# Linear attention mixer: scored queries turned back by four transpositions against a reordered identity

## What is computed

```python
def step(S, inp):
    qc, kc, vc, gc = inp                        # chunks of 16 positions
    G = jnp.cumsum(gc, axis=1)
    qg = qc * jnp.exp(G)
    att = jnp.einsum('blhd,bshd->bhls', qg, kc * jnp.exp(-G))
    att = jnp.where(causal, att, 0.0)
    o = jnp.einsum('bhls,bshv->blhv', att, vc) + jnp.einsum('blhd,bhdv->blhv', qg, S)
    g_last = G[:, -1]
    S = S * jnp.exp(g_last)[..., None] + jnp.einsum('bshd,bshv->bhdv', kc * jnp.exp(g_last[:, None] - G), vc)
    return S, o
```

## Time and profile before

| what | before |
|---|---|
| median of 3 runs | 2017.05 us (2014.43, 2017.05, 2022.57) |
| span of the profiled execution, the only time the profile gives for it | 2015.7 us |
| TensorE busy (matrix passes) | 1951.5 us, 97% |
| TensorE busy (weight loads) | 1763.9 us, 88% |
| VectorE, ScalarE, GpSimd busy | 62%, 46%, 50% |
| DMA | 324.64 MB, mean 161 GB/s |

### The profile page before, as it was taken

One profiled execution on the slowest core, in us unless ns is written; L12 is line 12 of the kernel. 1 busy time (PEld: TensorE's weight loads), 2 busy tenths in 40 slices (PEclk: granted clock), 3 DMA queues, 4 the chain that ended last, 5 costly groups with the idle time before them and its releaser, 6 DMA issues.

```text
span 2015.7 us, 35615 instructions
## 1 busy us (share of the span) xinstructions
PE 1951.5 (97%) x13890; PEld 1763.9 (88%) x13890; DVE 1244.4 (62%) x2220; ACT 930.6 (46%) x1557; POOL 1008.8 (50%) x1249
## 2 busy tenths in 40 slices
PE   7999999999999999999999999999999999999997
PEld 5998989798888988897889999999998889989976
DVE  5988342426887787755147777777454157874552
ACT  3676522334555555342354444443243347674333
POOL 4776704026555655250356666566631337776602
PEclk8999999999999999999999999999999999999998
DMA  4444476535444544487353444444586344445870
GB/s 130 149 147 135 135 250 231 208 105 174 124 116 132 151 132 140 138 297 241 113 170 108 130 130 130 137 136 146 165 313 211 132 148 141 135 148 166 292 231 27
DMA packets 332615, 324.64 MB, mean 161 GB/s; under 512 B 19768, under 2 KB 313056, under 8 KB 332448
## 3 DMA queue, kind: packets, MB, share of 16 engines
q1 hardware_dynamic: 330944, 321.49, 49.8%
q10 hardware_dynamic: 1504, 0.87, 0.2%
HBM read 292.16 MB, written 29.61 MB: 160 GB/s over the span
## 4 chain that ended last, share of the span: by engine, by line
PE 75%; DVE 14%; ACT 5%; issue 2%; DMA 2%; POOL 1%; SPq 1%; DVEq 0%; ACTq 0%
PE ps L773 10%; PE ps L774 10%; PE ps L778 10%; PE ps L1458 5%; PE ps L1467 4%; PE ps L1261 3%; PE ps L1524 2%; PE ps L888 2%; PE ps L763 2%; PE ps L765 2%; PE ps L764 2%; ACT wh L1713 2%; DVE work L2543 2%; PE ps L1602 1%; PE ps L1541 1%
## 5 line engine op out<-in xcount | busy, mean ns | idle before, releaser
L1693 POOL TENSOR_TENSOR wl<-raw,wh 128x256 fp32r<-128x256 f32 x1216 | 1003.3, 860 | 979.1 <-ACT wh L1713 978.9
L1713 ACT ACTIVATE wh<-raw 128x1024 fp32r<-128x1024 f32 x304 | 311.8, 1053 | 202.1 <-PE ps L778 49.8
L773 PE MATMUL ps<-Hh,wh 128*128 128x320 f32 x1200 | 372.2, 324 | 2.8 <-DVE work L2563 0.9
L774 PE MATMUL ps<-Hl,wh 128*128 128x320 f32 x1200 | 360.4, 314 | 0.0
L773 PEld LDWEIGHTS ps<-Hh,wh 128*128 128x128 f32 x1200 | 230.0, 192 | 11.3 <-DVE work L2427 2.3
L774 PEld LDWEIGHTS ps<-Hl,wh 128*128 128x128 f32 x1200 | 230.4, 192 | 2.1
L2258 DVE TENSOR_SCALAR work<-ps 128x512 f32<-128x512 f32 (+8 forms) x220 | 100.3, 474 | 170.9 <-PE ps L871 39.8
L778 PE MATMUL ps<-Hh,wl 128*128 128x320 f32 x1200 | 201.1, 310 | 0.0
L778 PEld LDWEIGHTS ps<-Hh,wl 128*128 128x128 f32 x1200 | 183.2, 189 | 0.1
L773 PE MATMUL ps<-Oh,wh 128*128 128x320 f32 x512 | 152.2, 310 | 3.7 <-DVE Ol L3004 3.7
L774 PE MATMUL ps<-Ol,wh 128*128 128x320 f32 x512 | 151.1, 308 | 0.0
(11 more groups left out here) (439 smaller groups left out, 3922.0 us busy)
## 6 DMA issues: line engine op xcount, KB each, us to landing
raw<-rg_w_in SPq DMA_DIRECT2D x128, 256.0 KB, 3.5
raw<-hg_w_in SPq DMA_DIRECT2D x128, 256.0 KB, 4.8
raw<-ssd_w_in SPq DMA_DIRECT2D x96, 256.0 KB, 3.9
work<-cache_mem_k SPq DMA_DIRECT2D x40, 512.0 KB, 6.3
work<-cache_mem_v SPq DMA_DIRECT2D x40, 512.0 KB, 5.1
raw<-rg_w_out SPq DMA_DIRECT2D x64, 256.0 KB, 3.6
raw<-x_w_k SPq DMA_DIRECT2D x64, 256.0 KB, 3.6
raw<-x_w_v SPq DMA_DIRECT2D x64, 256.0 KB, 3.7
```

The source lines that it names most:

```text
L773: pe.matmul(ps[:, bank, 0:n], high(half, k), mh[:, k, 0:n], start=(k == 0), stop=False)
L774: pe.matmul(ps[:, bank, 0:n], high(half, k), ml[:, k, 0:n], start=False, stop=False)
L1693: ins = pool.tensor_tensor(out, src, wh[:, parted(n) % HALVES, r:r + 2].bitcast(F32), ALU.subtract)
L1713: act.activation(wh[:, nx.n % HALVES], raw[:, slot, :, half * P:(half + 1) * P], ACT.Copy).then_inc(hi_ready, 1)
```

## The change

The four products of line 1302 become four transpositions (one line further down, line 1303, since a line is added). Each writes 128 columns in place of 64. The columns of the identity are reordered, so that the 64 wanted ones come first and the 64 unwanted ones behind them; the next product starts 64 columns further on and overwrites the unwanted ones. For that the high half is now done before the low one in each tile. The unwanted columns of the last tile are columns 256 to 319 of bank 4, of which the samples' product overwrites partitions 0 to 63. Number and place of the instructions in the program, waits and signals stay as they are.

```diff
-                    own = ident[:].rearrange("p (g r) -> p g r", g=4)[:, :, 0:16]
+
+                    own_first = ident[:].rearrange("p (g a r) -> p a g r", g=4, a=2)
                     for T in range(2):
-                        for low in range(2):
+                        for low in (1, 0):
                             at = T * P + 64 * (1 - low)
-                            pe.matmul(ps[:, 4, at:at + 64], hg_sq[:, T, P * low:P * low + P], own, start=True, stop=True)
+                            pe.matmul(ps[:, 4, at:at + P], hg_sq[:, T, P * low:P * low + P], own_first, start=True, stop=True, is_transpose=True)
                     pe.matmul(ps[0:64, 4, 256:320], hg_ks[:, h, :], hg_q[i % 2][:, h, SEQ:NT], start=True, stop=True).then_inc(S("hg_att_full"), 1)
```

## The result

| | before | after |
|---|---|---|
| median of 6 runs | 2016.18 us (2012.97 to 2022.57) | 2003.13 us (2000.39 to 2006.66) |
| ratio | | 0.9939, 95% interval 0.9923 to 0.9955 |
| span of the profiled execution | 2015.7 us | 2001.6 us |
| stretches at granted clock 0.50 inside the mixer ("slow stretches") | 9 | 4 |

The change makes the kernel 13 us faster, 0.6%, against 5.2 us forecast and a range that ended at 2004.5. I start where the page of the changed kernel differs.

What follows compares the result with a forecast made beforehand. PE's instruction stream was taken to bound the mixer. 6.4 us saved by sixteen shorter turnings back, less 1.2 us lost at waits, gives 5.2 us: 2017.05 - 5.2 = 2011.8 us, range 2004.5 to 2019.0.

Steps and rivals of the forecast that it cites:

- The price of the instructions: Turning back in the mixer: four transpositions take 0.53 us against 0.93, saving 0.40 us per head, 6.4 us for sixteen.
- The dear and the cheap end of the bounds: Price of a transposition in the turning back: 0.22 us each saves 1.1 us in all, 0.055 us each saves 9.0.
- the clock: Half-clock stretches in the mixer, 1.5 us each, get redrawn: three more or fewer, 4.5 us either way, middle unmoved.
- What is given back: PE arrives earlier at three waits for the weights' low part in the mixer: 3 x 0.40 = 1.2 us lost.
- transpositions count as rest: Rival: turning back draws new half-clock stretches; eight give 2023.9 us, sixteen 2035.9. Chance 0.10, 0.04 for over 0.5%.
- the passes would be as dear as before: Rival: new transpositions take two passes each or stall on overlapping columns; gain 1.1 us or less, 2016 us. Chance 0.10.
- the chain binds in every period: Rival: the states' chain bounds every mixer period, 3.2 us waited away, 3.2 left: 2013.9 us. Chance 0.10.
- More than forecast: Rival: cheap end's 9.0 us, or 5.2 us plus three half-clock stretches fewer, 9.7: 2007.4 us. Chance 0.13.

Runs made afterwards that it cites:

- the clear pair: Kernel before and changed kernel, each with 8-column products filled to 32 columns and SyncE's weight block ahead of the store: 1998.01 us and 1993.66 us.
- the 64-column run: Kernel before with the samples' 8 products of 8 columns widened to 64 columns each: 2007.2 us, ratio 0.9952.
- moving the load: Changed kernel with SyncE issuing the fourth weight block of a group ahead of the store of head 1's states: 2000.04 us, ratio 0.9921.
- the changed kernel with both edits: Changed kernel with 8-column products filled to 32 columns and SyncE's weight block ahead of the store: 1993.66 us, ratio 0.9891.
- the widened changed kernel: Changed kernel with the samples' 8-column products widened to 64 columns: 2002.6 us, ratio 0.9921.

## Why the prediction was right or wrong

**The price of the instructions was right.** Starts 0.11 us apart, 0.53 us in all, 6.4 us for sixteen; the clear pair shows 6.3. The dear and the cheap end of the bounds were both wrong. The factor of four that I quoted from the Trainium skill ("TensorE: Matmul & The Clock Gate", section "Terms"), read as four against the same product, isn't what these rows show: a transposition in float32 takes 0.11 us, half of the 0.22 of a two-pass product.

**The step that failed is the clock.** It stood in the sum with nothing and was allowed 4.5 us either way; it measured 7.5 us. I wrote that "shifting PE by 0.4 us a head will redraw them", three more or fewer, and that it "doesn't move its middle". I treated the nine stretches as a draw with the same mean before and after. They have different means: 9 and 12 in the old loop, 4 and 5 in the new, five fewer by the granted clock of all executions as well, which is 7.5 us, more than the instructions gave. I had the mechanism (the thin groups), the price (1.5 us, confirmed by the 64-column run) and the number of stretches, and did not ask whether the number is a property of the loop. A loop that repeats its stream eight times, two heads each, may well repeat its bad place too. What could have been said blind is that the clock's term had no known sign and reached from 0 to 13.5 us in gain, since up to nine stretches could go; the range should have reached to about 1998.

**What is given back was wrong in sign.** I took 1.2 us off for three waits. That the wait has the chain of the earlier trace rows behind it was right, as moving the load showed. But in the profile after the waits are 1.7 us fewer, not 1.2 more. No run shows why: the waits do grow where slow stretches are taken away with nothing else changed (6.2 to 7.9 us and 4.5 to 8.6 us with 64 columns), but from the kernel before to the changed one both fell. Two profiles of one kernel differ by 0.5 (6.2 and 6.7) and 0.8 us (4.5 and 5.3), so a term of 1.2 us is near what can't be told apart.

**The rivals.** That transpositions count as rest fell: with eight transpositions a head the clock is what it was, and the changed kernel with both edits has no slow stretch in the mixer. The rule of the Trainium skill behind it ("TensorE: Matmul & The Clock Gate", "Part 4: PE-mode transpose") shows nowhere in these traces. That the passes would be as dear as before fell with the starts. That the chain binds in every period was nearly seen once the stretches were gone: the widened changed kernel waited in six places for the low weights. "More than forecast" had the right mechanism, three stretches fewer, and 2007.4 us; it was five.

**What stays open.** Why a turning back of 0.53 us places the thin groups well, and one of 0.75 as badly as one of 0.93, isn't shown. The runs show that the length of the loop's stream decides and that half of the shortening brings nothing of the clock's part. That the place in time is what the length changes is theory A; what speaks for it is that 64 of the 68 slow stretches in the mixers with 8-column products begin 0.3 to 1.5 us behind the start of a group's last pass, but no run set the place alone. Which length is best can't be read from them.

## What to carry to other kernels

Where the granted clock is below 1.00 in a stretch in which PE never rests, look for runs of passes with few columns just ahead of each drop, and price them apart from the instructions: here a drop cost 1.5 us, and the number of drops changed by five when 0.40 us per head went. Such a kernel can't be judged by a change of passes alone; first fill the thin passes (they took 1.81 to 1.83 us with 32 or 64 columns and 1.81 with 8), and then measure the change. Don't take the number of drops for chance, or for a property of the kernel, before the mean granted clock of many executions and a variant of another length have been compared.

## What the runs showed of the hardware that was not expected

- The clock falls to 0.50 though PE had no gap ahead of it, as in the earlier trace rows. Of the sixteen groups of 8-column passes (1.81 us each) 2 to 13 drew a slow stretch at once, by kernel and execution. With 32 or 64 columns in about the same time none did: 0 slow stretches in the mixer in four of the five kernels that had them, 1 in the other, 8.5 us behind its group.
- Four of the 68 slow stretches came 9 us behind a thin group, each behind a wait of PE of 1.8 to 2.7 us.
- Passes of 8, 32 and 64 columns with a new stationary operand each occupy PE equally long, 0.11 us (sixteen in 1.81, 1.81 and 1.83 us).
- A permuted identity serves a transposition at no cost, and writes that overlap those of the pass before cost nothing either: 0.53 us from the first of four to the samples' product, as the key transpositions would have it.
